# Even layer: all late taps inside the three state-space turns, the output of three groups as longer products in the last group; four norms worked by tiles in the layer in front

## The chip, the core and the metric

The kernel is one program on one core of a Trainium2 chip. The metric is device time in microseconds: the median of three runs, taken beside one profiled execution. The core has five engines with queues of their own, which meet only at semaphores: TensorE (PE in the rows: matmuls and transposes into PSUM), VectorE (DVE), ScalarE (ACT: activation functions, from tables that are loaded when the function changes), GpSimd (POOL) and SyncE (SP: it issues the weight loads). Each engine works its own queue in order, so an instruction that waits holds up everything behind it on its engine.

## The reference

Six layers run one after another on an activation x of 512 tokens by 1024 features. Each normalises x, projects it, mixes, gates, projects back and adds the result to x. The first block has pool, gdn, mla and pool layers and ends with a norm; the second block has an even and an odd layer. All is float32. The part that matters here is the even layer:

```python
hn = rmsnorm_2(x, norm_w)
z_a, xbc, dt_raw, glu_v, glu_g, z_b = split(hn @ w_in)
xbc = silu(causal_dwconv(xbc, conv_w, conv_b))          # 4 taps
y = ssd_chunked(xs, dt, a, bs, cs, d_skip) * silu(z_a)  # 4 groups of 4 heads
y_a = rmsnorm_2 of each group of 256 features
u = causal_dwconv(glu_v * sigmoid(glu_g), dw_w, dw_b)   # 31 taps, 1024 channels
y_b = silu(layernorm(u)) * silu(z_b)
return x + concatenate([y_a, y_b]) @ w_out              # w_out: 2048 x 1024
```

and `rmsnorm(x, g) = x * rsqrt(mean(x * x) + 1e-6) * g` in front of every layer.

## The kernel before

**Layout and products.** x stands transposed in `xT`: eight tiles of 128 features by 512 tokens. Every large product is made of three fp32r matmuls (L310 to L312), of the high and low part of the activation (`xh`, `xl`) with the high and low part of the weights (`whi`, `wlo`). `product` (L293) does the k steps k0 to k1 of one 128x512 output tile into one of four rotating PSUM banks; a k step is three matmuls. Small work uses the other four banks (`wbank`).

**Weights.** SyncE loads slots of up to 128x1024 into a ring of four (`load_slot`), ScalarE rounds one to its high part (`slot_hi`, L276), GpSimd subtracts in four pieces (`slot_lo`, L291). `hi_after(sec, i, j)` on ScalarE does the high parts of the slots that may follow once slot j is used; each waits for the last matmul of the slot that held its place. The items of SLOTS give each slot's shape as (k steps, tiles): (8, 1) is one tile of eight k steps, (4, 2) two tiles of four. `ring_positions` gives the places; where the count isn't a multiple of four the last slots use three of them. The even layer has 65 slots: 49 for the inputs, then 4 (4, 2), 8 (8, 1) and 4 (4, 2) for the outputs.

**Norms.** `norm` (L386) serves five layers. ScalarE and VectorE first wait for the last tile's add to x (`x_ready[-1][-1]`). ScalarE squares the tiles (L394) into two buffers; VectorE makes `xh` (L415) and `xl` (L418) of tile after tile; in `first_product` TensorE does one k step and one fp32 matmul with ones (L404, the sum of squares, two records) in turn. Then ScalarE makes `R` (L397 Ln, L400 Exp, a table load before each). `R` is multiplied in only where a product leaves PSUM, so products may run ahead of it. The even layer has a norm of its own, two norms in one (`tail_vector`, `tail_scalar`, `sums_tensor`, `norms_scalar`, `norms_vector`, L719 to L775): its squares already run tile by tile in the pool layer in front, through the table `tails`; `sums` collects squares of tiles 0 to 6, and TensorE adds them up after the last output product. The table DMAs of a layer (`tables`) are issued by ScalarE before its norm.

**The even layer's order, written by hand.** (1) 25 products for the gated unit, with the 31-tap convolution on VectorE, one instruction a tap (L816). Channel tiles are called c = 0 to 7; of the odd ones only the first 13 taps (EARLY) are done here. (2) Six input products of group 0, `in_at(0, 0..5)`; `first_tap` on ScalarE, `other_taps` on VectorE (L972, three instructions a tile, the last frees the product's bank) and `conv_silu` (L980) are its 4-tap convolution. Behind each `other_taps` stand late taps of channel tiles 1 and 3. (3) Three turns: `work_tensor(i)`, `work_scalar(i)`, `work_vector(i)` are the state-space work of group i, and between its small steps TensorE does pieces (two k steps, six matmuls) of group i+1's six input products, 24 pieces. `more(n)` places n of them: 3 behind the x transposes (L1012), 1 behind each of three state products, 2 behind each head's row product (L1033), 1 behind each head's y, one more ahead of the last head's y (L1056, L1057), 4 ahead of the y sums (L1044), and what is left behind them. Head h on ScalarE is Exp, four Relu, Exp; on VectorE the product with C (L1126) and the mask product M h (L1129), for which y head h waits. `between(p)` on either engine places other work: p = 0 to 2 around the states, 3 + h behind M h on VectorE and 1 + h behind head h on ScalarE, then 7 (VectorE) and 5 (ScalarE) around the group norm. VectorE puts the late taps of tiles 5 and 7 there, 12 a turn. The four `conv_silu` of group i+1 stand at the end of ScalarE's turn. (4) The last group: the same with the layer norm of the 31-tap convolution's result (L1158 to L1208) in the places, and as pieces the output products of groups 0 and 1, 16 pieces, two for a tile; VectorE adds tiles 0, 1 at p = 2 and then two each at p = 3, 4, 5. Behind it: eight products of the second half (OUTB, 64 k steps), and eight tiles of groups 2 and 3 (OUT23, 32 k steps).

## Time and profile before

| | |
|---|---|
| median of 3 runs | 2914.63 us (2914.26 to 2919.36) |
| the profiled execution | 2915.16 us |
| its span, first to last instruction | 2913.4 us |
| mean granted TensorE clock | 0.968 |
| TensorE busy with matmuls | 2709.3 us, 93% |
| VectorE, ScalarE, GpSimd busy | 1637.2, 1024.8, 1135.8 us |

The layers' places in the span: the first pool layer to 337 us, gdn to 1024, mla to 1657, the second pool layer to 1978, even to 2494, odd to the end. Inside the even layer, 2154.0 to 2192.3 is the stretch before the turns, from there to 2250.3 turn 0, to 2307.5 turn 1, to 2365.5 turn 2 with the mean, to 2427.2 the last group, to 2494.1 the rest. A time in a timeline is counted from the span's first instruction. "Idle before" is how long the engine stood still before an instruction, and the releaser is what ended that. The granted clock is a share of full speed: 1.0 is 2.4 GHz, 0.5 is 1.2 GHz, and a mean between them says how much of a stretch was at the lower level.

### The profile page before, as it was taken

Reading aid. Unit: us, or ns where it says so; the run is one execution under the profiler, and the core shown is the slowest. Engines: PE = TensorE matmul, PEld = TensorE weight load, DVE = VectorE, ACT = ScalarE, POOL = GpSimd, SP = SyncE. Lnnn points to the kernel's source line nnn. Section 1 sums busy time; section 2 is a strip of 40 time slices with the busy share of each in tenths; the row PEclk is TensorE's granted clock in tenths of the full one; section 3 lists DMA queues with packets and bytes.
Section 4 is the critical chain, followed back from the end, with each engine's and each line's share of the span. In section 5 each row is a group of like instructions: output and inputs, shape, how many; then the busy total and the mean of one; then the engine's idle time right before and its main releaser. Section 6 shows DMA issues by size and latency. Waiting matters only on the chain.

```text
span 2913.4 us, 34384 instructions
## 1 busy us (share of the span) xinstructions
PE 2709.3 (93%) x12132; PEld 2103.5 (72%) x12132; DVE 1637.2 (56%) x2729; ACT 1024.8 (35%) x1456; POOL 1135.8 (39%) x1445
## 2 busy tenths in 40 slices
PE   8999979999999788999999899998988998989996
PEld 6888758888888566777777588886866666656673
DVE  6655466665565433444443655566996653356565
ACT  2222233333333233333333322225424563335443
POOL 5666433233232133333334256664543323423320
PEclk9999989999999899999999999999998998989998
DMA  3222211111111011112221132222221111211110
GB/s 127 97 94 94 85 66 51 58 58 51 55 53 44 29 58 67 60 59 67 67 67 60 66 102 94 94 95 73 94 72 58 53 49 51 93 37 59 64 37 29
DMA packets 56797, 195.71 MB, mean 67 GB/s; under 512 B 6384, under 2 KB 8944, under 8 KB 56688
## 3 DMA queue, kind: packets, MB, share of 16 engines
q1 hardware_dynamic: 55536, 192.90, 19.7%
q10 hardware_dynamic: 1152, 1.38, 0.2%
q8 instruction: 67, 1.10, 0.2%
q14 instruction: 42, 0.34, 0.0%
HBM read 192.15 MB, written 2.10 MB: 67 GB/s over the span
## 4 chain that ended last, share of the span: by engine, by line
PE 83%; DVE 10%; ACT 4%; issue 2%; DMA 0%; POOL 0%; SPq 0%; ACTq 0%; DVEq 0%
PE psum L310 21%; PE psum L312 21%; PE psum L311 21%; PE psum L1635 4%; PE psum L404 1%; PE psum L2236 1%; PE psum L2210 1%; PE psum L2211 1%; DVE psum L816 1%; DVE e_c L816 1%; PE psum L2548 1%; PE psum L1641 1%; DVE xT L434 1%; ACT whi L276 1%; PE psum L1704 1%
## 5 line engine op out<-in xcount | busy, mean ns | idle before, releaser
L291 POOL TENSOR_TENSOR wlo<-raw,whi 128x256 fp32r<-128x256 f32 x1436 | 1135.4, 822 | 1716.1 <-ACT whi L276 1716.0
L310 PE MATMUL psum<-xh,whi 128*128 128x512 f32 x1832 | 779.5, 425 | 31.0 <-POOL wlo L291 10.5
L312 PE MATMUL psum<-xh,wlo 128*128 128x512 f32 x1832 | 723.0, 395 | 0.0
L311 PE MATMUL psum<-xl,whi 128*128 128x512 f32 x1832 | 722.8, 395 | 0.0
L276 ACT ACTIVATE whi<-raw 128x1024 fp32r<-128x1024 f32 (+1 forms) x365 | 377.4, 1042 | 915.6 <-PE psum L312 914.9
L310 PEld LDWEIGHTS psum<-xh,whi 128*128 128x128 f32 x1832 | 350.4, 191 | 136.2 <-issue 53.3
L311 PEld LDWEIGHTS psum<-xl,whi 128*128 128x128 f32 x1832 | 350.4, 191 | 79.4 <-issue 16.5
L312 PEld LDWEIGHTS psum<-xh,wlo 128*128 128x128 f32 x1832 | 348.7, 190 | 76.3
L434 DVE TENSOR_TENSOR xT<-psum,xT 128x512 f32<-128x512 f32 x192 | 130.1, 689 | 210.0 <-PE psum L312 209.6
L312 PE MATMUL psum<-pool_yh,wlo 128*128 128x512 f32 x256 | 101.5, 397 | 0.0
L310 PE MATMUL psum<-pool_yh,whi 128*128 128x512 f32 x256 | 101.5, 396 | 0.0
L311 PE MATMUL psum<-pool_yl,whi 128*128 128x512 f32 x256 | 101.5, 396 | 0.0
L527 DVE TENSOR_TENSOR pool_u<-psum,R 128x512 f32<-128x512 f32 x32 | 22.1, 691 | 132.4 <-PE psum L312 132.4
L2167 DVE TENSOR_TENSOR mwork<-psum,R 128x512 f32<-128x512 f32 x16 | 11.1, 691 | 122.9 <-PE psum L312 122.9
L816 DVE SCALAR_TENSOR_TENSOR psum<-e_ue,par,psum 128x512 f32<-128x512 f32 x112 | 79.6, 742 | 0.0
L2278 DVE TENSOR_REDUCE mxs<-psum 128x1 f32<-128x128 f32 (+1 forms) x64 | 31.3, 489 | 79.8 <-PE psum L2212 79.8
L1577 DVE SCALAR_TENSOR_TENSOR stg<-pre,par,stg 128x512 f32<-128x512 f32 x96 | 72.7, 757 | 3.2 <-DVE stg L1573 0.9
L2247 ACT ACTIVATE mwork<-psum,nmx 128x128 f32<-128x128 f32 (+1 forms) x64 | 33.8, 528 | 107.8 <-DVE nmx L2280 107.8
L310 PE MATMUL psum<-cqh,whi 128*128 128x512 f32 x144 | 61.1, 425 | 4.7 <-issue 4.7
L2162 ACT ACTIVATE mwork<-psum 128x512 f32<-128x512 f32 x48 | 26.8, 595 | 102.0 <-PE psum L312 89.6
L310 PE MATMUL psum<-gyh,whi 128*128 128x512 f32 x128 | 54.6, 426 | 5.4 <-DVE gyl L1868 5.4
L312 PE MATMUL psum<-cqh,wlo 128*128 128x512 f32 x144 | 57.5, 399 | 0.0
(493 smaller groups left out, 4693.5 us busy)
## 6 DMA issues: line engine op xcount, KB each, us to landing
raw<-weights_dram SPq DMA_DIRECT2D x341, 512.0 KB, 3.3
raw<-weights_dram SPq DMA_DIRECT2D x24, 384.0 KB, 3.0
xin<-x_dram SPq DMA_DIRECT2D x4, 512.0 KB, 6.3
out_dram<-y SPq DMA_DIRECT2D x4, 512.0 KB, 2.6
g_masks<-gdn_masks_dram ACTq DMA_DIRECT2D x1, 384.0 KB, 2.9
par<-params_dram SPq DMA_DIRECT2D x1, 319.5 KB, 3.2
mwork<-positions_dram ACTq DMA_DIRECT2D x1, 256.0 KB, 2.9
o_pT<-positions_dram ACTq DMA_DIRECT2D x1, 256.0 KB, 3.3
```

The source lines that it names most:

```text
L276: act.activation(whi[:, q, 0:nk * nm * P], raw[:, q, 0:nk * nm * P], ACT.Copy).then_inc(hi_ready[q], 1)
L291: last = pool.tensor_tensor(wlo[:, q, part], raw[:, q, part], whi[:, q, part].bitcast(F32), ALU.subtract)
L310: pe.matmul(gbank(b), whi[:, q, c:c + P], h, start=k == 0, stop=False)
L311: pe.matmul(gbank(b), whi[:, q, c:c + P], l, start=False, stop=False)
L312: done = pe.matmul(gbank(b), wlo[:, q, c:c + P], h, start=False, stop=k == nk - 1)
L404: pe.matmul(wbank(0), ones, sq[:, k % 2, :], start=k == 0, stop=k == KD - 1)\
L434: dve.tensor_tensor(xT[:, t, :], tile(sec, j, m), xT[:, t, :], ALU.add).then_inc(*taken(sec, j, m))
L816: dve.scalar_tensor_tensor(out=out, in0=src[:, k:k + SEQ], scalar=w, in1=old, op0=ALU.mult, op1=ALU.add).then_inc(*ve.done(f"tap {c} {k}"))
L1577: dve.scalar_tensor_tensor(out=stg[:, x, :], in0=pre[:, x, tap:tap + SEQ], scalar=w, in1=stg[:, x, :], op0=ALU.mult, op1=ALU.add)\
L1635: last = pe.matmul(wbank(b)[:, c * P:(c + 1) * P], left[:, c, :], right[:, c, :], start=True, stop=True)
L2247: act.activation(prob[:, hd, off_q[t]:off_q[t] + w], wbank(x % 4)[:, 0:w], ACT.Exp, scale=SCALE, bias=nmx[:, x:x + 1], accum_out=rs[:, x:x ...
L2278: dve.reduce_max(mxs[:, x:x + 1], wbank(x % 4)[:, 0:w], AX.X).then_inc(*ve.done(f"max raw {x}"))
```

## The change

In the even layer, no late taps stand before the turns; all 72 go into the three turns, 24 in each, at p = 0 to 7. `conv_silu` of the next group moves from the end of ScalarE's turn to p = 4, behind the fourth head. The output of groups 0 to 2 becomes one run of eight tiles of six k steps, (6, 1), done as 24 pieces in the last group; the counts in `work_tensor` stay. VectorE adds two tiles at p = 2, two at p = 3, one each at p = 4, 5 and 6 and the last behind the group. ScalarE's `hi_after` for the new slots stands at p = 1 (two), 2 (one), 3 (two), 4, 5 and behind the group. Group 3's output remains at the end: 16 k steps in two slots of (2, 4). The layer has 67 slots.

`norm` is split into a step for each tile, which the layer in front calls through `behind`: ScalarE makes `xh` (now a Copy with the gain as scale) and the square behind the tile's add; VectorE makes `xl` of the tile before, ahead of the next add; TensorE does the sum of squares of tile m-3 behind output tile m. ScalarE waits before a square for the sum (or add) that frees its buffer. `first_product` does the sums that are left. With `summed` (the gdn layer) VectorE adds the squares into `Rt` and TensorE has two sums, behind the product. Table DMAs go behind the tiles' steps (`then`). The even layer's own norm: its squares go ahead of the weights' `hi_after`, its two sums over tiles 0 to 5 behind output tile 6, the last tile's first square goes to VectorE.

```diff
+        def norm(n, gain, summed=False):
...
+            def tile_scalar(act, m):
+                emitted["scalar"] = m + 1
+                act.wait_ge(*before[m])
+                act.activation(xh[:, m, :], xT[:, m, :], ACT.Copy, scale=gain[:, m:m + 1]).then_inc(*ae.done(f"hi {m}"))
+                if m >= 2:
+                    act.wait_ge(*(ve.of(f"summed {max(1, m - 2)}") if summed else te.of(f"sum {m - 2}")))
+                act.activation(sq[:, m % 2, :], xT[:, m, :], ACT.Square).then_inc(*ae.done(f"square {m}"))
...
+            def tile_vector(dve, m):
+                emitted["vector"] = m + 1
+                if m:
+                    lo(dve, m - 1)
+                if summed and m >= 2:
+                    dve.wait_ge(*ae.of(f"square {m - 1}"))
+                    if m > 2:
+                        dve.wait_ge(*ve.of(f"summed {m - 2}"))
+                    dve.tensor_tensor(Rt[:, :], sq[:, 0, :] if m == 2 else Rt[:, :], sq[:, (m - 1) % 2, :], ALU.add)\
+                       .then_inc(*ve.done(f"summed {m - 1}"))
...
+            def tile_tensor(pe, m):
+                if not summed and m >= 3:
+                    sum_squares(pe, m - 3)
...
+                if summed:
+                    pe.wait_ge(*ve.of(f"summed {KD - 2}"))
+                    pe.matmul(wbank(0), ones, Rt[:, :], start=True, stop=False)
+                    pe.wait_ge(*ae.of(f"square {KD - 1}"))
+                    pe.matmul(wbank(0), ones, sq[:, (KD - 1) % 2, :], start=False, stop=True)\
+                      .then_inc(*te.done(f"sum {KD - 1}"))
...
+            def tail_tensor(pe, m):
+                if m == KD - 2:
+                    pe.wait_ge(*ve.of(f"summed {KD - 3}"))
+                    pe.matmul(wbank(1), ones, sums[:, 0, :], start=True, stop=False)
+                    pe.matmul(wbank(1), ones, sums[:, 1, :], start=False, stop=False)
...
-            def late_taps(dve, a, k0, k1):
-                for k in range(k0, k1):
+            def late_taps(dve, q0, q1):
+                for q in range(q0, q1):
+                    a, k = 1 + 4 * (q // (TAPS - EARLY)), EARLY + q % (TAPS - EARLY)
...
                 def end_pieces():
-                    hi, lo = [yh[:, k, :] for k in range(4)], [yl[:, k, :] for k in range(4)]
+                    hi = [yh[:, k, :] for k in range(4)] + y_rows(2)[0]
+                    lo = [yl[:, k, :] for k in range(4)] + y_rows(2)[1]
                     for m in range(KD):
-                        for k in (0, 2):
-                            product(pe, *out_at(OUT01, m), hi, lo, [ve.of(f"{k // 2} y lo {k % 2}") for k in range(4)],
+                        for k in (0, 2, 4):
+                            product(pe, S, 0, OUTA + m, 0, hi, lo, [ve.of(f"{k // 2} y lo {k % 2}") for k in range(6)],
                                     k, k + 2)
                             yield
...
+                        if p == 4:
+                            for a in range(4):
+                                conv_silu(act, i + 1, a)
...
+                    for m in {1: (0, 1), 2: (2,), 3: (3, 4), 4: (5,), 5: (6,)}.get(p, ()):
+                        hi_after(act, S, 0, OUTA + m, True)
                     if 1 <= p <= 4:
-                        hi_after(act, S, 0, OUT01 + p - 1, True)
...
-                    k = EARLY + 6 * i
                     def between(p):
-                        if p == 1:
-                            late_taps(dve, 5, k, k + 1)
                         if 3 <= p <= 6:
                             other_taps(dve, i + 1, p - 3)
-                            late_taps(dve, 5, k + p - 2, k + p - 1)
-                        if p == 7:
-                            late_taps(dve, 5, k + 5, k + 6)
+                        first, count = {0: (0, 1), 1: (1, 1), 2: (2, 1), 3: (3, 1), 4: (4, 2), 5: (6, 1), 6: (7, 2),
+                                        7: (9, 3)}.get(p, (0, 0))
+                        late_taps(dve, 12 * i + first, 12 * i + first + count)
...
                     if p == 2:
-                        add(OUT01, 0)
-                        add(OUT01, 1)
+                        for m in range(2):
+                            add_tile(dve, S, 0, OUTA + m, 0, m)
...
+                add_tile(dve, S, 0, OUTA + 7, 0, 7)
                 for m in range(KD):
                     add_tile(dve, S, 0, OUTB + m, 0, m)
                 for m in range(KD):
-                    add(OUT23, m)
+                    behind("vector", dve, n, m)
+                    add_tile(dve, *out3_at(m), m)
...
-    "even": [("even", 1, [(8, 1)] * 49 + [(4, 2)] * 4 + [(8, 1)] * 8 + [(4, 2)] * 4)],
+    "even": [("even", 1, [(8, 1)] * 49 + [(6, 1)] * 8 + [(8, 1)] * 8 + [(2, 4)] * 2)],
```

Not shown: the same calls of `behind` in the gdn and mla layers (ScalarE: `behind` for four tiles, then `hi_after`; VectorE: `behind`, then `add_tile`; TensorE: `behind` after each tile of the last section), and the weights' order in memory.

## Rows read from the trace of the kernel before

**Rows 1.** The page, part 1: busy us of each engine, share of the span, instructions.
```profile
PE 2709.3 (93%) x12132; PEld 2103.5 (72%) x12132; DVE 1637.2 (56%) x2729; ACT 1024.8 (35%) x1456; POOL 1135.8 (39%) x1445
```

**Rows 2.** What TensorE waited for: us in total, times, the longest.
```profile
PE psum L1012 <- ACT e_stg L980: 12.7, 1, 12.7
PE psum L310 <- POOL wlo L291: 10.5, 2, 5.4
...
PE psum L1550 <- DVE Q L1521: 9.8, 1, 9.8
PE psum L996 <- ACT e_stg L980: 8.2, 2, 4.1
PE psum L1057 <- DVE e_D L1129: 8.2, 2, 7.9
PE psum L2129 <- ACT sq L2115: 8.1, 2, 6.8
PE psum L310 <- DVE xl L418: 7.9, 3, 2.6
...
PE psum L1044 <- ACT e_ecs L1080: 5.1, 1, 5.1
...
PE psum L741 <- DVE e_gp L727: 3.8, 1, 3.8
```

**Rows 3.** Timeline, even to odd: start, us, engine, line, what [idle before, releaser].
```profile
2494.03 0.69 DVE L434 TENSOR_TENSOR xT<-psum,xT 128x512 f32<-128x512 f32 x1 [2.09 <-PE psum L312]
...
2508.38 1.02 PE L404 MATMUL psum<-sq,cst 128*128 128x512 f32 x2
...
2509.93 1.02 PE L404 MATMUL psum<-sq,cst 128*128 128x512 f32 x2
...
2512.98 0.63 ACT L400 ACTIVATE R<-Rt 128x512 f32<-128x512 f32 x1
```

**Rows 4.** Timelines, pool to gdn: the splits, and ScalarE to `R`.
```profile
337.14 1.06 ACT L276 ACTIVATE whi<-raw 128x1024 fp32r<-128x1024 f32 x1 [20.48 <-PE psum L312]
...
338.28 7.88 POOL L291 TENSOR_TENSOR wlo<-raw,whi 128x256 fp32r<-128x256 f32 x8 [16.87 <-ACT whi L276]
...
359.29 0.63 ACT L400 ACTIVATE R<-Rt 128x512 f32<-128x512 f32 x1
```

**Rows 5.** One line's instructions, the taps: duration min/median/max in ns, first and last start.
```profile
L816 DVE SCALAR_TENSOR_TENSOR e_c<-e_uk,par,e_c x72: 737/744/1224, 2157.1 to 2349.1; 128x512 f32<-128x512 f32 x72
```

**Rows 6.** Stretches: us, busy PE, PEld, DVE, ACT, POOL (instructions), PEclk, DMA share, GB/s.
```profile
2154.00:2192.30 38.30, 20.29 (x83) 16.32 (x82) 37.98 (x49) 8.98 (x13) 13.21 (x13) 0.75 0.12 41
2192.30:2250.30 58.00, 53.90 (x239) 40.21 (x239) 37.12 (x54) 30.68 (x53) 20.82 (x26) 0.94 0.17 55
...
2307.50:2365.50 58.00, 57.78 (x255) 40.68 (x254) 34.47 (x50) 30.84 (x53) 20.58 (x28) 1.00 0.17 55
2365.50:2427.20 61.70, 48.43 (x187) 31.08 (x187) 40.29 (x59) 42.88 (x65) 16.09 (x17) 0.88 0.11 35
2427.20:2494.10 66.90, 66.80 (x288) 54.49 (x287) 14.26 (x22) 15.31 (x18) 28.22 (x40) 0.98 0.25 81
```

**Rows 7.** VectorE before the turns: first set in the timeline; late taps as a group.
```profile
2154.88 2.31 DVE L972 SCALAR_TENSOR_TENSOR e_stg<-psum,par,e_stg 128x511 f32<-128x511 f32 x3
...
L816 DVE SCALAR_TENSOR_TENSOR e_c<-e_uk,par,e_c 128x512 f32<-128x512 f32 x35 | 29.7, 918 | 0.0
```

**Rows 8.** Timeline, end of turn 0 on VectorE and ScalarE.
```profile
2241.53 1.42 DVE L1144 SCALAR_TENSOR_TENSOR e_xd<-e_xd,par,Rt 128x512 f32<-128x512 f32 x2 [6.13 <-ACT Rt L1085]
...
2244.93 2.56 ACT L980 ACTIVATE e_stg<-e_stg,par 128x512 f32<-128x512 f32 x4
```

**Rows 9.** Timelines, last group: M 1 and M 3 on VectorE, ScalarE's load for head 2.
```profile
2394.90 0.69 DVE L1129 TENSOR_TENSOR e_D<-e_D,e_cbm 128x512 f32<-128x512 f32 x1 [1.00 <-ACT e_D L1075]
...
2414.30 0.69 DVE L1129 TENSOR_TENSOR e_D<-e_D,e_cbm 128x512 f32<-128x512 f32 x1 [1.00 <-ACT e_D L1075]
...
2400.99 1.28 ACT L1068 ACT_TABLE_LOAD   x1
```

More of the change, by code:

```diff
@@ L423, in norm, with between @@
-            return {"scalar": scalar, "vector": vector, "steps": {"scalar": [ae], "tensor": [te], "vector": [ve]},
-                    "first product": first_product}
+                first = emitted["tensor"]
+                def between(k):
+                    if not summed and k >= first:
+                        sum_squares(pe, k)
+                for k in range(KD):
+                    product(pe, sec, i, j, 0, xh, xl, [ve.of(f"lo {k}") for k in range(KD)], k, k + 1)
+                    between(k)
@@ L426, in add_to_x, with behind @@
+            tails[n] = {"scalar": tile_scalar, "vector": tile_vector, "tensor": tile_tensor}
+            return {"scalar": scalar, "vector": vector, "first product": first_product, "then": then}
+        def behind(engine, eng, n, m):
+            if n + 1 in tails:
+                tails[n + 1][engine](eng, m)
         def add_to_x(dve, sec, i, j, tiles):
@@ new lines, in sums_tensor @@
+            def sums_tensor(pe):
+                b = (KD - 2) % 2
+                pe.wait_ge(*ae.of(f"squares {KD - 2}"))
+                for q in range(2):
+                    pe.matmul(wbank(1), ones, stg[:, b, q, :], start=False, stop=False)
+                pe.wait_ge(*ae.of(f"squares {KD - 1}"))
+                pe.matmul(wbank(1), ones, stg[:, 1 - b, 1, :], start=False, stop=False)
+                pe.wait_ge(*ve.of("scaled last"))
+                pe.matmul(wbank(1), ones, stg[:, 1 - b, 0, :], start=False, stop=True).then_inc(*te.done("both norms"))
@@ L743, in sums_tensor @@
                 pe.matmul(wbank(0), ones, sums[:, 0, :], start=True, stop=False)
-                pe.wait_ge(*ae.of(f"squares {last}"))
-                pe.matmul(wbank(1), ones, stg[:, last % 2, 0, :], start=False, stop=False)
-                pe.matmul(wbank(1), ones, stg[:, last % 2, 1, :], start=False, stop=True).then_inc(*te.done("both norms"))
-                pe.matmul(wbank(0), ones, stg[:, last % 2, 0, :], start=False, stop=True).then_inc(*te.done("first norm"))
+                pe.matmul(wbank(0), ones, stg[:, b, 0, :], start=False, stop=False)
@@ L749, in norms_scalar @@
+                pe.matmul(wbank(0), ones, stg[:, 1 - b, 0, :], start=False, stop=True).then_inc(*te.done("first norm"))
             def norms_scalar(act):
@@ L1928, in scalar @@
                 for j in (0, 1):
+                    for m in range(4 * j, 4 * j + 4):
+                        behind("scalar", act, n, m)
                     hi_after(act, last_sec, 0, j, True)
@@ L2348, in scalar @@
                 for j in (0, 1):
+                    for m in range(4 * j, 4 * j + 4):
+                        behind("scalar", act, n, m)
                     hi_after(act, last_sec, 0, j, True)
@@ L2910, in slot_sources @@
             yield from tiles(w[:, g * 256:(g + 1) * 256])
-        yield from tiles(out[0:512], 256)
+        yield from tiles(out[0:768])
         yield from tiles(out[1024:2048])
-        yield from tiles(out[512:1024], 256)
+        yield from tiles(out[768:1024], 512)
     if kind == "odd":
```

143 lines of the change are left out of this document (75 added, 68 removed).

## The prediction, made before the changed kernel was seen

> **What bounds the kernel now.** I read the page first: TensorE is busy 93% of the span [rows 1]. The other engines can only cost time where TensorE stands still, so I listed what TensorE waited for, in time order against the code. It stands still about 204 us (span less busy), in few places, and those the change touches are in [rows 2]: 12.7 us before the token transposes ahead of the first turn of the even layer; 4.1 us twice at the head of turns 1 and 2 (the 8.2 us on L996); 7.9 and 5.1 us in the last group; and one stall at every layer boundary (2.65 us on `xl` L418 three times, 5.1 us on the weight split, 3.8 us on the sums of the even layer). Two more, 9.8 us on `Q` and 6.8 us on `sq`, come later than a boundary but end a chain that begins with its `R`. A stall costs more than its length: the granted clock is 0.75 over the stretch before the turns, 0.94 over turn 0 with its one 4.1 us stall, and 1.00 over turn 2 with none [rows 6]. So in turn 0 6% of 58 us, 3.5 us, are lost to the 1.2 GHz level behind the stall.
>
> I sum against the profiled execution: 2915.2 us with a span of 2913.4 us, 0.5 us above the median of the runs, 2914.6. A measurement of this kernel tells about 0.2% (6 us) from no change.
>
> **Four norms by tiles.** Today a boundary goes: last add, split into `xh` and `xl`, and a first product whose eight k steps each take 1.55 us, for each is three matmuls and one fp32 sum (L404, start to start) [rows 3]. A matmul of a dense product costs 66.8/288 = 0.23 us [rows 6], so a k step is 0.70 us and a sum 0.86 us. From the last tile to the end of the sums it is 2494.0 to 2510.9 us, 16.9 us, and `R` ends at 2513.6, 19.6 us behind the tile [rows 3]. After: squares and splits of tiles 0 to 6 run beside the output products, and sums 0 to 4 stand between them. Four of these push the last tile back by 3.4 us, then come sum 4, eight k steps and three sums: 0.86 + 5.6 + 2.6 = 9.1 us. Together 12.5 us instead of 16.9.
> - mla to pool: nothing waits for `R` at once, TensorE gains the 4.1 us that its first product ends earlier.
> - gdn to mla, even to odd: what waits is `R` (6.8 us on `sq` [rows 2]). ScalarE now waits in square 7 for sum 5 inside the first product, and behind that wait stand the splits of the next weights, two table DMAs and a table load. That takes back 1 us at mla (one split of 1.05 us) and 1.5 us at odd (two). Gains 3.5 and 2.9 us. The DMAs are late by 9 us, and land before `R`.
> - pool to gdn: the first gdn slot reuses the place of the last output slot. Its hi split starts at 337.1 us, and VectorE-disturbed lo pieces of 0.98 us each (7.88/8) let the product start 5.1 us after the last tile [rows 2, 4]. ScalarE now does the last tile's add-wait, copy and square (2.0 us) first; but VectorE is free by then and a piece takes 0.7 us, so the product starts 1 us late. It then runs 5.4 + 1.8 (slow clock) + 1.7 us (two sums instead of eight, as VectorE adds the squares) = 8.9 us from 343.1, and with Ln, load and Exp (2.6 us) `R` ends at 354.7 instead of 359.9 [rows 4]. Gain 5 us, carried to the 9.8 us stall on `Q` [rows 2].
> - pool to even: the 3.8 us stall [rows 2] goes, two sums move ahead of the last tile (+1.7, +0.7 of waiting), two fewer stand behind it. Gain 3.9 us.
> - load to pool: same norm, nothing in front of it; 0.
>
> Sum of the boundaries: 4.1 + 3.5 + 2.9 + 5.0 + 3.9 = 19.4 us.
>
> **The stretch before the turns.** VectorE is busy 37.98 of 38.3 us, TensorE 20.29 [rows 6]. Behind each of the four sets of `other_taps` stand late taps, 36 in all, 35 of them in this window, 29.7 us [rows 7]; the convolution's last SiLU, and with it the transposes, wait for them. Taken out, the sets follow one another (2.3 us each, the first from 2154.9 to 2157.2 [rows 7]), the last, with ScalarE's first taps between, is done at 2164.3, and TensorE is the bound again: two products of 5.6 us from the first bank freed, to 2168.6, then transposes and the masks' product (2.6 us) to 2171.2. Today this point is at 2192.2, the window's end. With the 0.9 us of slow clock behind the old stall: gain 21.9 us. The bound below is 17, should ScalarE's order (split, first tap, SiLU) come last.
>
> **The turns.** They take 12 more late taps each. A tap costs 0.74 us alone (0.70 in a row of them) and 1.22 at worst [rows 5]; 12 x 0.70 = 8.4 us. VectorE is busy 37.1 of 58 us in turn 0 [rows 6], so it has room. Most added taps fall in idle time: two pairs behind the `y z` products stand before a wait of 6.1 us for `Rt` [rows 8]; where a pair delays a head's mask product, TensorE still has pieces for 4 to 7 us. And the SiLUs leave the end of the turn: there a table load, then four activations from 2244.9, held the transposes 4.1 us [rows 2, 8]. At the fourth head they cost one more load (1.28 us) in ScalarE's idle time. What is late next is VectorE's `y lo`, done as the first state product needs it. Gain per change of turn 4.1 us and the slow clock behind it: 6.7 and 5.0, together 11.7 us (bounds 4 and 14). Turn 2 is followed by the mean, without a stall: 0.
>
> The Trainium skill speaks against this step ("SBUF — State Buffer", section "Who interferes with whom"): a VectorE instruction with two SBUF inputs and a GpSimd instruction that reads SBUF exclude each other. The late taps are of that form, and the 1.22 us in [rows 5] agrees. It is rival B.
>
> **The last group.** Work of TensorE moves in: 24 pieces of six matmuls instead of 16, so 8 x 1.39 = 11.1 us less behind the group, and 13.0 us of stall to fill [rows 2]. But the call counts of the pieces are unchanged, and a tile is three pieces, not two. Tile 4 is complete only with piece 15, behind y head 1; tile 5 with 18, behind y head 2; tile 6 with 21, behind y head 3. VectorE's adds of 4, 5 and 6 are queued right behind the mask products of heads 1, 2, 3, and behind each add stand the `ln_y` that ScalarE's `ln_hi` waits for before it can begin the next head. Today no add waits. Step by step: M 1 (the mask product of head 1) today ends at 2395.6, M 3 at 2415.0, 9.7 us for each head [rows 9]; add 3 now waits for piece 12 (2396.3), so M 1 ends at 2398.3. y head 1 (1.7), piece 14, row 3 (1.1), piece 15: add 4 at 2404.2, `ln_hi` 1 ends at 2406.8 against 2401.0 [rows 9], and with load, exponentials and mask (4.4 us) M 2 ends at 2411.2, 5.9 us late. The next loop, with y head 2 at half clock (3.3 us), has M 3 at 2425.2, 10.2 us late. Then y head 3 (3.3), pieces 19 to 21 (4.9), add 6, four products (2.5), skip and gate (2.1), a square: the y sums start at 2438.7, 15.3 us late, and with two pieces behind them, which are among the eight, the out products of the second half start some 17.4 us later. 11.1 - 17.4 = **-6.3 us**. Bounds: +6 (the waits don't bind, the pieces fill the stalls) and -10.
>
> **Sum.** 19.4 + 21.9 + 11.7 - 6.3 = 46.7; 2915.2 - 46.7 = 2868.5 us.
>
> **Rivals.**
> A. The last group gains: if the adds find their tiles done, 11.1 us leave and some 5 come back from ScalarE's longer head (two more splits). +6 instead of -6.3: 2856 us. For it: TensorE is 13 us idle there. Against: the order of the pieces.
> B. The late taps meet GpSimd's splits in the turns. All 24 of a turn at 1.22: 12 x 1.22 + 12 x 0.48 = 20.4 us more, 37.1 + 20.4 = 57.5 of VectorE against turns of 53: 4.5 us over, three times, 13.5 us: 2882 us. For it: before the turns the mean is 0.918 [rows 7]. Against: GpSimd works in a third of a turn (20.8 of 58) [rows 6].
> C. The norms give nothing, as ScalarE's waits for sums and its late splits eat the 19.4: 2888 us. That would be half the change not doing what it says.
> D. Slower: in the turns each head's mask product waits behind added taps, so that every added tap stands on TensorE's path at 1.22, 36 x 1.22 = 44 us, and 12 stalls each bring the low clock, 2.3 us each, 28 us: 2868.5 + 72 = 2940 us. It decides from 46.7/36 = 1.3 us of path per added tap. Against: a turn has one stall today and 21 us of VectorE idle.
>
> **How the numbers follow.** Forecast 0.50, A 0.19, B 0.20, C 0.06, D 0.03, and 0.02 that B, C and the last group's loss join to within 0.2%. The range from 2854 to 2888 holds the forecast with its bounds, A and B. Faster 0.95, same 0.02, slower 0.03.
>
> **What would show it.** Right: no 12.7 us wait on L1012 and the transposes some 21 us nearer to the last conv; no L996 waits; TensorE waiting for `e_D` at heads 2 and 3 of the last group for 5 to 8 us each, with VectorE's L434 there waiting for a product; boundaries of 12.5 us from tile to sums. Wrong: L1057 waits for `e_D` inside turns 0 to 2 (B, D), the last group's adds without a wait (A), or a stall at L404 for `sq` (C).

## The result and the profile after

| | before | after |
|---|---|---|
| median of the runs on one chip | 2915.61 us (2914.26 to 2919.36) | 2869.99 us (2867.40 to 2873.89) |
| after / before | | 0.984, 95% interval 0.983 to 0.985 |
| the profiled execution, its span | 2915.16, 2913.4 us | 2873.89, 2872.1 us |
| mean granted TensorE clock | 0.968 | 0.973 |

The change makes the kernel 46 us faster. The profiled execution of after is the slowest of its four, 3.9 us above the median. The page's first part, against [rows 1], shows TensorE busy for 12 us less and standing still for 29 us less. Of the 12 us some 2.6 are three sums of squares fewer (six records), at the prediction's 0.86 us a sum; the rest is the higher clock:

```profile
PE 2697.4 (94%) x12126; PEld 2097.3 (73%) x12126; DVE 1597.4 (56%) x2695; ACT 1054.5 (37%) x1500; POOL 1124.0 (39%) x1445
```

The stretches of the even layer, as [rows 6]: us, busy PE, PEld, DVE, ACT, POOL, PEclk, DMA share, GB/s. In this order: before the turns, turns 0, 1 and 2, the last group to the y sums, and from there to the last output product.

```profile
2120.50:2158.80 38.30, 38.01 (x178) 31.50 (x177) 31.95 (x48) 14.77 (x21) 19.41 (x29) 1.00 0.29 96
2158.80:2209.60 50.80, 50.80 (x240) 37.66 (x239) 40.44 (x60) 27.75 (x48) 16.51 (x21) 1.00 0.16 53
2209.60:2260.40 50.80, 50.80 (x239) 37.66 (x239) 43.16 (x63) 31.45 (x53) 20.68 (x25) 1.00 0.18 63
2260.40:2318.00 57.60, 57.60 (x255) 40.64 (x254) 44.86 (x65) 34.86 (x58) 23.72 (x27) 1.00 0.17 55
2318.00:2393.70 75.70, 57.30 (x218) 39.05 (x217) 35.18 (x55) 42.09 (x65) 16.66 (x20) 0.87 0.13 42
2393.70:2458.70 65.00, 64.98 (x265) 50.82 (x266) 22.04 (x30) 23.58 (x30) 31.07 (x40) 0.96 0.21 73
```

Up to the last group TensorE no longer stands still: busy 38.01 of 38.30 us where [rows 6] has 20.29, and 50.80 of 50.80 in each of two turns. In the last group it stands still for 18.4 us. What TensorE waited for (us in total, times, the longest), the rows that answer to [rows 2]; L1121 and L1108 are the last group:

```profile
PE psum L1121 <- DVE e_D L1193: 14.0, 3, 7.0
...
PE psum L1614 <- DVE Q L1585: 9.8, 1, 9.8
PE psum L2199 <- ACT sq L2185: 8.2, 2, 6.8
...
PE psum L310 <- DVE xl L404: 6.8, 1, 6.8
...
PE psum L310 <- POOL wlo L291: 5.9, 1, 5.9
...
PE psum L1108 <- ACT e_ecs L1144: 4.4, 1, 4.4
...
PE psum L792 <- DVE e_gp L777: 1.8, 1, 1.8
```

The waits on the transposes (L1012, L996 of before) are gone; L1121 is the line of L1057. The wait on L404 is the one behind the load of x, where TensorE waited 5.4 us in before; the three boundary waits on `xl` [rows 2] are gone. VectorE in the timeline of the last group says where its 14.0 us come from:

```profile
2349.09 0.69 DVE L482 TENSOR_TENSOR xT<-psum,xT 128x512 f32<-128x512 f32 x1 [5.99 <-PE psum L312]
2349.69 1.05 DVE L1190 TENSOR_TENSOR e_ecs<-e_ecs,e_stg 128x512 f32<-128x512 f32 x1
2350.66 1.21 DVE L1193 TENSOR_TENSOR e_D<-e_D,e_cbm 128x512 f32<-128x512 f32 x1
...
2357.94 0.69 DVE L482 TENSOR_TENSOR xT<-psum,xT 128x512 f32<-128x512 f32 x1 [4.87 <-PE psum L312]
2358.55 1.28 DVE L1268 TENSOR_TENSOR e_c<-e_c,e_zs 128x512 f32<-128x512 f32 x2
...
2364.13 0.69 DVE L1193 TENSOR_TENSOR e_D<-e_D,e_cbm 128x512 f32<-128x512 f32 x1 [1.00 <-ACT e_D L1139]
...
2372.48 0.69 DVE L482 TENSOR_TENSOR xT<-psum,xT 128x512 f32<-128x512 f32 x1 [5.92 <-PE psum L312]
...
2378.67 0.69 DVE L1193 TENSOR_TENSOR e_D<-e_D,e_cbm 128x512 f32<-128x512 f32 x1 [1.00 <-ACT e_D L1139]
...
2387.99 0.69 DVE L482 TENSOR_TENSOR xT<-psum,xT 128x512 f32<-128x512 f32 x1 [6.89 <-PE psum L312]
```

L482 is `add_tile`. Four adds wait for a tile that isn't complete, 23.7 us in all. Behind the first stands M 1 itself (L1193), behind the others `ln_y` (L1268), for which ScalarE waits before it starts the next head, so M comes 13.5 and 14.5 us after the one before, where it was 9.7 us [rows 9]. ScalarE's own waits in the last group, down to the y sums, show this link:

```profile
ACT xh L1254 <- DVE e_c L1268: 17.3, 3, 6.9
```

L1254 is `ln_hi`. In before the same wait is 2.6 us in all.

**Where the time went.** I cut each span at the same events: the end of each `R`, the first product of the even layer, the end of the token transposes of each group, the last output product. Lengths in us; "4 sums" marks the 3.4 us of sums that after has ahead of the last output product and before has behind it, counted back in the last column.

| stretch | before | after | gain | after, second execution |
|---|---|---|---|---|
| start to `R` of the first pool layer | 36.0 | 38.2 | -2.2 | 36.7 |
| to `R` of gdn | 323.9 | 319.5 | 4.4 | 318.7 |
| to `R` of mla | 683.7 | 678.9 | 4.8 | 678.4 |
| to `R` of the second pool layer | 633.3 | 628.2 | 5.1 | 630.2 |
| to the first even product | 319.0 | 318.2 | 0.8 | 318.1 |
| to the transposes of turn 0 | 196.2 | 175.9 | 20.3 | 174.9 |
| turns 0, 1, 2 | 58.0, 57.2, 58.1 | 50.8, 50.8, 57.6 | 14.1 | 50.8, 50.8, 57.6 |
| last group to the last output product | 128.5 | 140.7 | -12.2 + 3.4 (4 sums) = -8.8 | 139.3 |
| to `R` of odd | 19.6 | 12.3 | 7.3 - 3.4 = 3.9 | 12.3 |
| to the end | 399.7 | 401.0 | -1.3 | 401.2 |

### The profile page after: what moved, and what is told of

The parts are those of the page before. It is cut to its first block, busy times and chain, and to the rows that moved or that the text cites. A ratio compares the mean times of both kernels' runs of the same rounds, so it can differ in the third digit from the quotient of the medians.

```text
span 2872.1 us, 34417 instructions
## 1 busy us (share of the span) xinstructions
PE 2697.4 (94%) x12126; PEld 2097.3 (73%) x12126; DVE 1597.4 (56%) x2695; ACT 1054.5 (37%) x1500; POOL 1124.0 (39%) x1445
## 4 chain that ended last, share of the span: by engine, by line
PE 85%; DVE 9%; ACT 3%; issue 2%; DMA 1%; POOL 0%; SPq 0%; ACTq 0%; DVEq 0%
PE psum L310 22%; PE psum L312 21%; PE psum L311 21%; PE psum L1699 4%; PE psum L2306 1%; PE psum L2280 1%; PE psum L2281 1%; DVE psum L878 1%; PE psum L2624 1%; PE psum L423 1%; DVE xT L482 1%; PE psum L1705 1%; PE psum L1768 1%; ACT whi L276 1%; PE psum L1121 1%
## 5 line engine op out<-in xcount | busy, mean ns | idle before, releaser
L291 POOL TENSOR_TENSOR wlo<-raw,whi 128x256 fp32r<-128x256 f32 x1436 | 1123.6, 815 | 1686.4 <-ACT whi L276 1686.4
L310 PE MATMUL psum<-xh,whi 128*128 128x512 f32 x1832 | 767.8, 419 | 18.6 <-DVE xl L404 6.8
L310 PEld LDWEIGHTS psum<-xh,whi 128*128 128x128 f32 x1832 | 349.0, 190 | 115.5 <-issue 42.5
L311 PEld LDWEIGHTS psum<-xl,whi 128*128 128x128 f32 x1832 | 348.9, 190 | 75.0 <-issue 11.6
L482 DVE TENSOR_TENSOR xT<-psum,xT 128x512 f32<-128x512 f32 x192 | 130.2, 688 | 194.7 <-PE psum L312 194.3
L2237 DVE TENSOR_TENSOR mwork<-psum,R 128x512 f32<-128x512 f32 x16 | 11.1, 692 | 122.9 <-PE psum L312 122.9
L2624 PE MATMUL psum<-o_kn,o_qz 128*128 128x128 f32 (+3 forms) x128 | 49.7, 479 | 8.4 <-ACT o_prob L2664 3.4
## 6 DMA issues: line engine op xcount, KB each, us to landing
par<-params_dram SPq DMA_DIRECT2D x1, 319.5 KB, 3.0
```

The lines of the kernel that those rows point to most:

```text
L291: last = pool.tensor_tensor(wlo[:, q, part], raw[:, q, part], whi[:, q, part].bitcast(F32), ALU.subtract)
L310: pe.matmul(gbank(b), whi[:, q, c:c + P], h, start=k == 0, stop=False)
L311: pe.matmul(gbank(b), whi[:, q, c:c + P], l, start=False, stop=False)
L482: dve.tensor_tensor(xT[:, t, :], tile(sec, j, m), xT[:, t, :], ALU.add).then_inc(*taken(sec, j, m))
L2624: pe.matmul(wbank(b)[:, 0:w], qz[:, hd, m, t * P:w], kn[:, hd, 0:w], start=True, stop=False)
```

## The experiments

The theory after the result: before the turns VectorE was the bound; in the turns the SiLUs were; the norms gain what moved ahead of the last tile; and the last group loses by the place of the adds alone. Each ratio is to the kernel before, measured on the same chip; before's own medians on the chips used lie between 2915.6 and 2919.9 us. Line numbers are those of after: L1044 is `conv_silu`, L1036 `other_taps`, L1076 and L1060 the transposes (L1012 and L996 of before), L1272 `ln_lo`, which is L1277 in run 10. "Last group" below means from its token transposes to the last output product.

**1. The adds one head later** (a tile is complete when VectorE comes to it).

```
-                        for m in {3: (2, 3), 4: (4,), 5: (5,), 6: (6,)}[p]:
+                        for m in {3: (2,), 4: (3,), 5: (4,), 6: (5,)}[p]:
...
                     if p == 7:
+                        add_tile(dve, S, 0, OUTA + 6, 0, 6)
```

> The changed kernel, but in the last group of the even layer VectorE adds each tile of the three-group products one head later (tile 2 behind M 0, 3 behind M 1, 4 behind M 2, 5 behind M 3, 6 behind the y z products). Theory (the adds were queued before their tiles were complete, and M of the next head, and the ln_y that ScalarE needs, stood behind them): the waits of L482 for TensorE (4.9, 5.9 and 6.9 us) go, the stalls of TensorE on e_D (1.5, 5.6 and 7.0 us) fall to about 3 us each or less, the y sums start 10 to 14 us earlier; about 2858 us. Rival (the head chain is ScalarE's own, longer by two weight splits; the adds only waited because there was time): the stalls stay within 1 us of 5.6 and 7.0 and the time stays at 2870 us.

2850.15 us, 0.977 of before (0.975 to 0.978): 20 us below the changed kernel. The theory holds, and the gain is larger than it said: the y sums start 57.8 us into the group, 16 to 18 us earlier, where 10 to 14 were expected, though one wait of 4.4 us on `e_D` is above the 3 us expected. The add's own row (line, ns min/median/max, first and last start), and what TensorE and ScalarE waited for in the last group:

```profile
L482 DVE TENSOR_TENSOR xT<-psum,xT x7: 677/679/683, 2325.9 to 2373.7; 128x512 f32<-128x512 f32 x7
...
PE psum L1121 <- DVE e_D L1193: 4.4, 1, 4.4
...
ACT xh L1254 <- DVE e_c L1268: 1.0, 2, 0.5
```

No wait is listed for L482 in that window, and ScalarE's 17.3 us of waiting have become 1.0, with the same weight splits on ScalarE: the head chain wasn't ScalarE's own, as the rival had it. The last group takes 120.4 us, where six executions with adds, outputs and norms as in the change (after, runs 3, 4, 5, 8 and 12) take 137.8 to 140.7: 14.0 us of waits less, and the rest, 3.5 to 6.4 us, is clock. Its windows, to the y sums and from there:

```profile
2316.50:2374.30 57.80, 53.25 (x220) 36.18 (x219) 37.80 (x55) 42.33 (x65) 20.83 (x20) 0.97 0.17 56
2374.30:2436.90 62.60, 62.60 (x266) 49.68 (x265) 22.15 (x31) 23.14 (x30) 31.08 (x40) 1.00 0.23 76
```

TensorE's busy time is 115.85 us against 122.28 in the changed kernel's profile, for the same matmuls: 6.4 us had been the low clock behind the waits in that execution, and 3.5 in the one where it cost least (run 8, 119.39).

**2. The output products as in the kernel before**: slots `[(4, 2)] * 4 + [(8, 1)] * 8 + [(4, 2)] * 4`, 16 pieces, the rest kept as changed.

> The changed kernel with the output products of the even layer as in the kernel before (16 pieces over two groups in the last group, the products of groups 2 and 3 at the end); taps, SiLUs and the four norms stay changed. Theory (the new layout costs 8.8 us from the start of the last group to the last tile): about 2861 us, y sums 15 to 18 us earlier behind the start of the last group. Rival (the layout itself gains, and what was lost comes from the SiLUs or taps moved in front of it): 2876 us.

2862.61 us, 0.981 (0.979 to 0.982). The last group takes 131.8 us, before's 128.5 and the four sums of 3.4. So the changed layout costs 139.0 (the mean of those six executions) less 131.8, 7.2 us; by the first execution of after 8.9. The last group starts no later here, so the rival (taps or SiLUs) is out. And it isn't the layout: with its adds placed as in 1 it gains 131.8 - 120.4 = 11.4 us: TensorE stands still for 4.6 us in place of 13.3, and 2.6 us are clock. The 11.1 us of work that it takes from behind the group nearly all went into time that was lost before.

**3. The late taps where they were.**

```
                 for a in range(4):
                     other_taps(dve, 0, a)
+                    late_taps(dve, 5 * a, min(5 * a + 5, 18))
...
-                        first, count = {0: (0, 1), 1: (1, 1), 2: (2, 1), 3: (3, 1), 4: (4, 2), 5: (6, 1), 6: (7, 2),
-                                        7: (9, 3)}.get(p, (0, 0))
-                        late_taps(dve, 12 * i + first, 12 * i + first + count)
+                        first, count = {1: (0, 1), 3: (1, 1), 4: (2, 1), 5: (3, 1), 6: (4, 1), 7: (5, 1)}.get(p, (0, 0))
+                        late_taps(dve, 18 + 6 * i + first, 18 + 6 * i + first + count)
```

> The changed kernel with the late taps where they stood before (36 between the sets of the first group, 12 in each turn). Theory (the stretch before the turns is bound by VectorE, and in the turns the added taps cost nothing): the wait of 12.7 us on the first transposes is back, 20.3 us lost there, the turns stay at 50.8 us; about 2890 us. Rival (half of the taps stand on the path in the turns too): the turns become 3 us shorter each, 2881 us.

2889.68 us, 0.990 (0.988 to 0.992). The stretch before the turns is 196.4 us long, as before the change (196.2), with its two waits:

```profile
PE psum L1076 <- ACT e_stg L1044: 12.6, 1, 12.6
PE psum L310 <- DVE e_stg L1036: 5.4, 2, 5.1
```

The turns are 51.6, 50.8 and 57.6 us: no shorter with half the taps. (TensorE doesn't stand still in any of them; the 0.8 us more in turn 0 is low clock behind the wait before it.) The taps' gain is the 20.5 us of that stretch alone, and in the turns the added ones cost nothing.

**4. The SiLUs back at the end of the turn.**

```
-                        if p == 4:
-                            for a in range(4):
-                                conv_silu(act, i + 1, a)
...
                     work_scalar(act, i, between)
+                    for a in range(4):
+                        conv_silu(act, i + 1, a)
```

> The changed kernel with the four SiLUs of the convolution back at the end of each turn. Theory (they held the transposes of the next turn 4.1 us, and the slow clock behind such a stall costs 2 to 3 us more): two stalls of 4.1 us, turns 0 and 1 of about 57.5 us, 2884 us. Rival one (only the stalls, no clock): 8.2 us, 2878 us. Rival two (the gain in the turns came from VectorE's new order of taps): no stall returns, 2870 us.

2885.19 us, 0.988 (0.987 to 0.990). Turns of 57.2, 57.9 and 58.6 us against 50.8, 50.8 and 57.6: 14.5 us, of which the waits are 8.2 and the clock behind them 6.3 (1.0 of it in the third turn, which has no wait):

```profile
PE psum L1060 <- ACT e_stg L1044: 8.2, 2, 4.1
```

**5. Half as many taps again in the turns**: behind each pair one more instruction of the same form, into a spare tile.

> The changed kernel with 12 further instructions of the late taps' form in each of the three turns, one behind each pair; they write to a spare tile (more work, same output). Theory (a tap lies in VectorE's idle time: 10.4 us of 50.8 idle in turn 0, 7.6 in turn 1, 12.7 of 57.6 in turn 2, against 9.1 us added): a loss of 0 to 5 us, mostly in turn 1; 2870 to 2875 us. Rival (each tap stands on TensorE's path through the mask products): 9 us a turn, 27 us, and stalls on e_D with slow clock behind them: 2900 us or more.

2881.03 us, 0.987 (0.986 to 0.989). The turns take 54.2, 55.4 and 61.3 us: 11.6 us more for 36 instructions, 0.32 us each, of which TensorE stands still for 9.6. Both expectations miss: the room was smaller than the idle time, since the instructions grew. VectorE over the three turns (us busy, mean ns, idle before it):

```profile
L878 DVE SCALAR_TENSOR_TENSOR e_c<-e_uk,par,e_c 128x512 f32<-128x512 f32 x72 | 54.6, 812 | 0.0
L1423 DVE SCALAR_TENSOR_TENSOR sq<-e_uk,par,xT 128x512 f32<-128x512 f32 x36 | 31.0, 887 | 0.0
...
L1190 DVE TENSOR_TENSOR e_ecs<-e_ecs,e_stg 128x512 f32<-128x512 f32 x12 | 12.5, 1043 | 0.6 <-ACT e_ecs L1132 0.6
```

The added ones took 0.887 us, not the 0.757 us that a late tap has in turn 0 of after. VectorE is idle for 30.7 of the 159.2 us of after's turns; the 36 added ones took 32, and the late taps and the products with C (L1190) 2.6 and 2.7 us more than in after. So the turns hold the 72 late taps but not half as many again; how many more would have been free isn't shown.

**6. Nothing ahead of the last tile** at four of the boundaries (the even layer keeps its own).

```
-            if n + 1 in tails:
+            if n + 1 in tails and plan[n + 1][0] == "even":
```

> The changed kernel, but at pool to gdn, gdn to mla, mla to pool and even to odd no square, split or sum is issued ahead of the last tile: the whole norm (still with the split on ScalarE) follows it. Theory (what the norms gain is the work moved ahead of the last tile): the boundaries give back 4.5 + 5.1 + 4.7 + 3.9 = 18 us, about 2888 us. Rival (part of the gain is the split that went from VectorE to ScalarE): 10 us or less, 2880 us.

2895.42 us, 0.992 (0.991 to 0.994): 25 us above the changed kernel, more than either expected. Against the first execution of after, the stretches to `R` of gdn, mla and pool are 7.1, 5.0 and 7.2 us longer, and the one to `R` of odd 8.7, less 3.4 for the sums. ScalarE behind the last tile of mla:

```profile
1664.12 1.06 ACT L276 ACTIVATE whi<-raw 128x1024 fp32r<-128x1024 f32 x1 [4.55 <-PE psum L312]
1665.08 0.71 ACT L396 ACTIVATE xh<-xT,par 128x512 fp32r<-128x512 f32 x1
1665.69 0.61 ACT L399 ACTIVATE sq<-xT 128x512 f32<-128x512 f32 x1
1666.21 0.71 ACT L396 ACTIVATE xh<-xT,par 128x512 fp32r<-128x512 f32 x1
```

The hi part, now ScalarE's, stands behind a weight split and alternates with the squares, and the first product waits 3.3 us for it.

**7. The same with the hi part on VectorE**, at the norm behind the load too, and the squares summed on TensorE at gdn: the norm as before the change.

> As the run with nothing ahead of the last tile (2895.4 us, 7 us above what the gains of the boundaries would give back), but with the hi part of the norms on VectorE and the squares summed on TensorE at all of them, as in the kernel before. Theory (behind the last tile hi stands on ScalarE behind a weight split and the squares, the first product starts 3.3 us after the tile in place of 2.65, and each tile's hi then waits its turn; so the split on ScalarE is worth its place only with work ahead): 6 to 8 us faster than that run, 2888 us. Rival (the 7 us have another cause, as the squares summed on VectorE at pool to gdn, or are noise): both runs within 2 us, or a gain at pool to gdn alone.

2887.93 us, 0.989 (0.988 to 0.991), 7.5 us under run 6; 1.5 of that stand at the load. The stretches are near those of before: 324.0 to `R` of gdn (323.9), 683.3 to mla (683.7), 634.8 to pool (633.3), 19.2 to `R` of odd (19.6). So the four norms are worth 17.3 us in the medians (less 2870.6 of run 12, on the same chip), or some 1 us more, since this kernel also has the faster norm at the load (run 8). The hi part on ScalarE with nothing ahead costs 2.6, 0.6, 0.6 and 1.8 us at the four boundaries; at the first, the other way to sum has a share in it that wasn't measured.

**8. Two small edits in one kernel**: the norm behind the load makes its hi part on VectorE again, and `tail_tensor` of the even layer issues its two sums at tile 7, behind the last product, in place of tile 6.

```
+                if n > 1:
+                    act.activation(xh[:, m, :], xT[:, m, :], ACT.Copy, scale=gain[:, m:m + 1]).then_inc(*ae.done(f"hi {m}"))
...
-                if m == KD - 2:
+                if m == KD - 1:
                     pe.wait_ge(*ve.of(f"summed {KD - 3}"))
```

> The changed kernel with two edits, 1.9 ms apart and read each from its own place: the norm behind the load of x makes its hi part on VectorE again, and at pool to even the two sums that stand ahead of the last output product go behind it. Theory for the first: hi stood on ScalarE behind four weight splits, R there ends 2.2 us earlier, at 36 us. Theory for the second: the wait of 1.82 us on L792 and 1.7 us of slow clock ahead of the last product go, and the first product of the even layer starts 3 to 4 us earlier. Together 5.5 us, 2864.5 us. Rival: the two sums add their 1.7 us behind the last tile, where nothing hides them: the second edit gives 1.8 us or less, together under 4 us.

2868.74 us, 0.983 (0.982 to 0.984). The median is 1.3 us under the changed kernel's first one and 1.9 under run 12's, where 5.5 were forecast and the rival said under 4; from the medians alone the two can't be told apart. By the stretches the second edit gains 2.4 or 4.0 us: from `R` to the first even product it is 314.15 us here and in both later kernels that have the edit, and 316.5 in six, 318.1 or 318.2 in four of the ten with the sums ahead. That is above the rival's 1.8 us, so the theory of the second edit holds in its own stretch; its size (3 to 4 us) is reached only against the four. The rows behind it, first of after, then of run 1, one of the six: in after the sums (L792, L793) wait and then run at half clock, and the first matmul of the last product too; in run 1 they wait as long and run at nearly full clock.

```profile
1964.70 2.02 PE L792 MATMUL psum<-e_gp,cst 128*128 128x512 f32 x2 [1.82 <-DVE e_gp L777]
1966.52 1.87 PE L793 MATMUL psum<-e_gp,cst 128*128 128x512 f32 x2
1967.44 1.18 PE L310 MATMUL psum<-pool_yh,whi 128*128 128x512 f32 x1
...
1965.77 1.13 PE L792 MATMUL psum<-e_gp,cst 128*128 128x512 f32 x2 [1.83 <-DVE e_gp L777]
1966.73 1.02 PE L793 MATMUL psum<-e_gp,cst 128*128 128x512 f32 x2
```

The load's edit starts the first product 4.8 us after the first weight split, in place of 6.0; it is 5.2 or 5.3 us in runs 7, 10 and 11, and 5.1 in before, so the edit is worth 0.7 to 1.2 us there. `R` comes at 36.1 to 37.3 us in four kernels with hi on VectorE there (runs 7, 8, 10, 11), and at 36.7 to 38.5 in nine with it on ScalarE: 0.9 us on average, under the 2.2 expected.

**9. Three more pieces ahead of y head 3**, on top of 1: `more(4)` there in the last group.

> The kernel with the adds one head later, and three more pieces of the three-group products ahead of y head 3. Theory (TensorE waits 4.45 us for M 3 there while six pieces of 1.4 us stand behind it): the wait goes, with it the slow clock behind it, 5 to 6 us; about 2844.5 us. Rival (the pieces missed behind head 3 leave a new wait before the y sums, for skip, gate and square): gain of 2 us or less, 2848 us.

2849.95 us, 0.976 (0.975 to 0.978): as run 1. The rival was right: of the wait of 4.45 us 0.3 are left, and another stands before the y sums:

```profile
PE psum L1108 <- ACT e_ecs L1144: 2.3, 1, 2.3
```

**10. All of it, with part of a second-half product in that gap** (k 0 to 5 of the first one).

> The changed kernel with the adds one head later, the norm behind the load and the two sums as in the earlier run of the two edits, and, in the last group, six of the eight k steps of the first second-half product (with the last pieces of the three-group products) between y head 3 and the y sums, where 2.3 us of waiting stood once three pieces had gone ahead of y head 3. Theory (each edit keeps its gain, for each is in another place: 22 us for the adds, 2 for the norm, 4 for the sums, 4 for the filled waits): 32 us under the changed kernel, 2840 us. Rival (the filling work runs out elsewhere: splits of the weights or lo parts of the second half are not ready, and a new wait stands before the first product of the second half): 2845 us or more.

2850.69 us, 0.977 (0.975 to 0.978): the rival again. What had been filled in came too early for its own operands:

```profile
PE psum L310 <- DVE xl L1277: 7.2, 2, 5.3
```

**11. The same, fitted to the lo parts.**

```
+                    if count == 5:
+                        half(0, 0, 4)
...
+                for m, k0, k1 in ((0, 4, 6), (1, 0, 6), (0, 6, KD), (1, 6, KD)):
+                    half(m, k0, k1)
+                for m in range(2, KD):
+                    half(m, 0, KD)
```

> As the run of all five edits, but with the second-half products fitted to when their lo parts come: four k steps of the first one (lo 0 to 3) between y head 3 and the y sums; behind the sums k 4 and 5 of it, k 0 to 5 of the second one, then k 6 and 7 of both. Theory (there TensorE waited 1.9 us for lo 4 or 5 and 5.3 us for lo 6, which stands on VectorE and ScalarE behind the norm of y, and the norm of y behind its sums): both waits go, with 1 to 3 us of slow clock behind them; 8 to 10 us under 2850.7, about 2842 us. Rival (the chain from y sums to lo 6 and 7 is the bound, and it ends no earlier): a wait of some 3 us or more on L310 for xl stays, 2846 us or more.

2845.70 us (2841.96 to 2846.26), 0.975 of before (0.973 to 0.976), 24 us below the changed kernel. The last group takes 115.5 us and TensorE is busy in nearly all of it:

```profile
2312.00:2370.00 58.00, 57.64 (x254) 39.81 (x253) 35.97 (x51) 42.31 (x65) 21.41 (x21) 1.00 0.18 56
2370.00:2433.00 63.00, 62.83 (x264) 48.95 (x263) 26.32 (x38) 26.07 (x34) 31.11 (x40) 1.00 0.27 90
```

The time is between the two expectations. The waits went as the theory says (9.1 us less in the last group); the other stretches came out 4 us longer than in run 10 with the same instructions, so that part is spread of the executions.

**12. The changed kernel once more**, beside 7, 10 and 11.

> The changed kernel itself, beside the others on one chip. Its profiled execution, 2873.9 us, was 3.9 us above the median of its runs; with the same stalls of 1.5, 5.6, 7.0 and 4.4 us another run had a last group 2.4 us shorter at a granted clock of 0.93 in place of 0.87. Theory: the low clock behind the same stalls lasts differently from one execution to the next; median 2870 us (0.984 of before), with last groups between 73 and 76 us.

2870.59 us, 0.983 (0.982 to 0.985). The last group to the y sums takes 74.9 us here, 75.7 in the first execution, and 73.3 to 75.5 in the other kernels with the same waits, as expected. Down to the last output product, in four of these executions:

```profile
2318.00:2458.70 140.70, 122.28 (x483) 89.86 (x483) 57.22 (x84) 65.67 (x94) 47.73 (x60) 0.92 0.17 57
2316.20:2455.50 139.30, 120.88 (x483) 89.06 (x482) 57.22 (x84) 65.71 (x94) 47.77 (x60) 0.94 0.18 57
2336.00:2474.00 138.00, 119.54 (x483) 87.87 (x482) 57.25 (x84) 65.71 (x94) 47.80 (x60) 0.95 0.17 58
2311.20:2449.00 137.80, 119.39 (x484) 87.81 (x483) 57.20 (x84) 65.66 (x94) 47.72 (x60) 0.95 0.18 58
```

The first is the changed kernel's first execution, the second this one, then runs 3 and 8. All four stand still for 18.4 us with the same work; what differs is the granted clock, 0.92 to 0.95, and by it 2.9 us of busy time.

## Why the prediction was right

2868.5 us were forecast and 2870.0 measured. The total is closer than its terms, and part of that is luck. The terms miss by up to 3 us either way and cancel only in part: the profiled pair moved by 41.3 us, 5.4 less than the 46.7 summed. The rest of the agreement is that the forecast starts from before's profiled execution and is compared with after's median, which lies 3.9 us under after's profiled one. The signs named as right came: the waits on L1012 and L996 are gone, `e_D` is waited for 5.6 and 7.0 us at heads 2 and 3 with the adds waiting for a product, and at even to odd it is 8.9 us from the last product to the end of the sums, with the 3.4 us ahead of it 12.3, where 12.5 were forecast.

- **The stretch before the turns**: 21.9 forecast, 20.3 in the profile, 20.5 by run 3. The chain that was named as next, TensorE's own work, is the one: busy 38.01 of 38.30 us. The gain is the two waits of run 3's rows (17.7 us) and the low clock behind them, 2.6 us more (TensorE busy 178.2 us in before from the first even product, 175.6 in after).
- **The turns**: 11.7 forecast, 14.1 measured, 14.5 by run 4. The mechanism is right; the clock term was too small. Behind each 4.1 us wait the low clock cost 3.1 us by run 4 (6.3 for two), where the forecast had 2.6 for turn 0 and 0.9 for turn 1. TensorE's busy time shows it: 53.9 us in turn 0 of before [rows 6] against 50.8 in after, so 3.1 us. Turn 1 of before had no row of its own in the working; it was guessed short.
- **The last group**: -6.3 forecast, -8.8 in the profiled pair, -7.2 over six executions, and the chain of causes as written: M 2, M 3 and the y sums were to be 5.9, 10.2 and 15.3 us late and were 7.0, 11.9 and 17.8 (their ends of 2364.8 and 2379.4 and the start of 2393.7, plus the 47.5 us by which this group starts earlier). What was short in that execution is the clock again: with the same waits the y sums of run 8 start 73.3 us into the group, 15.4 us behind before's 57.9, and those of after 75.7 us, 17.8 behind. Over the six executions the loss is 5.9 to 8.8 us, and the forecast lies inside. Rival A, which took the adds for ready, is refuted for this kernel; with the adds moved it comes true and better than its 2856 us.
- **The norms**: 19.4 forecast for five boundaries. By the table: pool to gdn 4.4 (5.0 forecast), gdn to mla 4.8 (3.5), mla to pool 5.1 and in the second execution 3.1 (4.1), even to odd 3.9 (2.9), pool to even 0.8 (3.9). The last is the step that failed. It counted 1.7 us for two sums and 0.7 of waiting ahead of the last product, 2.4 us. Counted from `R`, the last product ends at 301.0 us in before and in run 8, and at 304.8 in the six kernels of run 8's text and 306.4 or 306.5 in the four: 3.8 or 5.5 us later. The wait is 1.82 us in all ten, the sums 1.7, and the low clock behind them, which was not counted at all, 0.3 or 1.9. Behind the last product the stretch is 6.3 us shorter (18.0 to 11.7), as the 3.9 with its 2.4 has it, but not by "two fewer" sums: seven stand there where before had six (14 and 12 records of the trace). TensorE stands still for 5.6 us there in place of 10.9. With two sums of 0.86 us fewer the items as listed would also have given 3.1 us, not 3.9.
- **Load to pool**: 0 forecast, a loss of 0.7 and 2.2 in two executions. "Nothing in front of it" overlooked what a step that is moved to another engine meets there: four weight splits stand ahead of the hi part on ScalarE, and the first product starts 0.7 to 1.2 us later for it (run 8). Runs 6 and 7 show such a price at the other boundaries when no early tiles hide it, 5.6 us by the stretches.
- **Rival B** (added taps at 1.22 us): the late taps took 757, 793 and 778 ns on average in the three turns of after, 0.01 to 0.05 us above the median of before, 744 [rows 5]. Run 5 shows the effect when more are added: 0.887 us, and L1190 at 1.04 where it has 0.82 in turn 0 of after. The Trainium skill ("SBUF — State Buffer", section "Who interferes with whom") states that a VectorE instruction with two SBUF inputs and a GpSimd instruction that reads SBUF exclude each other. The trace agrees: of after's 72 late taps the 55 beside which no GpSimd instruction runs took 0.736 to 0.749 us each, and the 17 that overlap one 0.88 us on average and 1.222 at most. It weighs little, as GpSimd works in 61 of the 159 us of the turns. **Rival C** is refuted by run 7 (17 us), **rival D** by run 3: the turns don't get shorter without the added taps.

The range, 2854 to 2888, was set wide enough for rivals A (2856) and B (2882); the forecast's own terms miss by at most 3.1 us each.

## What to carry to other kernels

Place a transfer or add that empties a product's bank where its tile is already complete, counted in pieces of the producer's own order; one place too early cost 19 us here and turned a gain of 11 into a loss of 7. Count a stall of TensorE at its length and the low clock behind it (here 2.3 to 3.1 us behind 4.1 us waits, 0.3 or 1.9 behind one of 1.8), and look for such stalls also where sums are moved ahead of the work. When a step moves to another engine, list what already stands in that engine's queue at each place where the step occurs, the one place without early work among them. And when a gap is filled with later work, check when that work's operands come: nearly the same filler cost 7.2 us of waiting or 0.2, by its order.

## What the runs showed of the hardware

- The same instructions with the same waits take different time by the granted clock alone: 137.8 to 140.7 us for the last group, at 0.95 to 0.92. From `R` of the second pool layer to the first even product the ten kernels with the sums ahead of the last product took either 316.5 or 318.1 to 318.2 us, never a value between. TensorE stands still for 7.4 us in all ten; it is busy for 309.1 us in the six and for 310.7 or 310.8 in the four, and the same two sums behind the same wait of 1.8 us take 1.13 and 1.02 us in run 1, 2.02 and 1.87 in after. So the step of 1.6 us is the clock; what makes it fall in one execution and not in another isn't shown. So a difference of 2 us in one stretch of one execution shows nothing by itself, even where every wait is equal.
- A VectorE instruction of the late taps' form takes 0.74 us when no GpSimd instruction runs beside it and up to 1.22 when one does. In after's turns that makes 0.776 us on average over 72, in before's stretch ahead of the turns, where 17 of 35 overlap one, 0.918.
- An edit's gain in a median came out other than in its stretch (run 8: 1.3 us in the median, at least 2.4 in one stretch; run 11: 5.0 against 9.1 in the last group). For edits under 5 us the stretch over several kernels was the better witness.
